# Output projection of a hybrid encoder block: six of its eight chunks as seven block products

## The reference, cut to what matters

```python
D_MODEL, SEQ = 1024, 512
def layer(x):                                   # x: (512, 1024) float32
    h = rmsnorm(x, g_pre_mix)
    (..., gate_a, gate_b) = split_columns(h @ w_in)
    o_a, o_b = sparse_attention(...), stick_breaking_attention(...)
    m = (sigmoid(gate_a) * (o_a @ w_branch_sparse)
         + sigmoid(gate_b) * (o_b @ w_branch_sb))
    x = x + rmsnorm(m @ w_out, g_post_mix)      # <- the output projection
    h = rmsnorm(x, g_pre_ffn)
    g, u = split(h @ w_gate_up)
    return x + rmsnorm((silu(g) * u) @ w_down, g_post_ffn)
```

## Time and profile before

| | |
|---|---|
| median of three runs | 751.95 us |
| the profiled execution's own time | 751.47 us |
| its span, from first to last instruction | 749.7 us |
| PE busy | 741.4 us (99%) |
| DVE, ACT, POOL busy | 555.5, 427.9, 298.1 us |
| granted clock of TensorE, mean | 0.999 |

### The profile page before, as it was taken

How to read it: one execution, slowest core, us unless ns; L and a number is a source line. 1 busy time by engine, 2 the same in 40 slices (tenths; PEclk the granted TensorE clock), 3 DMA queues, 4 the chain that set the end, 5 groups by cost and what they waited for, 6 DMA issues and landing times.

```text
span 749.7 us, 11720 instructions
## 1 busy us (share of the span) xinstructions
PE 741.4 (99%) x4250; PEld 652.6 (87%) x4250; DVE 555.5 (74%) x781; ACT 427.9 (57%) x688; POOL 298.1 (40%) x213
## 2 busy tenths in 40 slices
PE   9999999999999999999999999999999999999996
PEld 7788888888888888888888989999999999788885
DVE  4979989977567565369607767778877777985778
ACT  5763177777677585643146454545554554655564
POOL 6937265966777878425382430000000000133102
PEclk9999999999999999999999999999999999999999
DMA  9652433213212232124553025323333314899902
GB/s 336 187 167 78 156 108 95 58 56 97 72 52 83 72 99 76 57 80 145 214 178 92 22 60 166 106 85 94 108 112 112 112 56 155 337 193 205 212 8 112
DMA packets 108977, 90.25 MB, mean 120 GB/s; under 512 B 3584, under 2 KB 91656, under 8 KB 108936
## 3 DMA queue, kind: packets, MB, share of 16 engines
q1 hardware_dynamic: 103752, 78.18, 33.3%
q0 software_dynamic: 4992, 11.54, 8.3%
q10 hardware_dynamic: 192, 0.01, 0.0%
HBM read 82.61 MB, written 3.68 MB: 115 GB/s over the span
## 4 chain that ended last, share of the span: by engine, by line
PE 95%; ACT 1%; DVE 1%; POOL 1%; issue 1%; DMA 0%; POOLq 0%; SPq 0%; ACTq 0%
PE ps L615 12%; PE ps L617 12%; PE ps L616 12%; PE ps L636 12%; PE ps L984 11%; PE ps L930 8%; PE ps L931 8%; PE ps L932 8%; PE ps L693 3%; PE ps L851 3%; PE ps L840 2%; PE ps L823 1%; PE ps L825 1%; ACT wr_hi L1436 1%; POOL x L1697 1%
## 5 line engine op out<-in xcount | busy, mean ns | idle before, releaser
L615 PE MATMUL ps<-h_hi,w_hi 128*128 128x512 f32 (+1 forms) x320 | 123.6, 386 | 0.0
L617 PE MATMUL ps<-h_hi,w_lo 128*128 128x512 f32 (+1 forms) x320 | 121.8, 381 | 0.0
L616 PE MATMUL ps<-h_lo,w_hi 128*128 128x512 f32 (+1 forms) x320 | 121.6, 380 | 0.0
L1688 POOL DMA_DIRECT2D w_a<-in_w_down x12 | 15.4, 1529 | 227.9 <-DVE xd_lo L2170 221.7
L1621 POOL TENSOR_TENSOR w_lo<-raw,w_hi 128x1024 fp32r<-128x1024 f32 x30 | 78.3, 2611 | 30.5 <-ACT w_hi L1180 30.1
L1505 POOL TENSOR_TENSOR w_lo<-raw,w_hi 128x1024 fp32r<-128x1024 f32 x20 | 48.7, 2441 | 58.1 <-ACT w_hi L1032 53.1
L617 PEld LDWEIGHTS ps<-h_hi,w_lo 128*128 128x128 f32 x320 | 60.2, 188 | 11.5
L616 PEld LDWEIGHTS ps<-h_lo,w_hi 128*128 128x128 f32 x320 | 60.4, 189 | 9.8
L615 PEld LDWEIGHTS ps<-h_hi,w_hi 128*128 128x128 f32 x320 | 60.3, 188 | 9.8
L2165 DVE TENSOR_TENSOR wr_lo<-w_a,wr_hi 128x1536 fp32r<-128x1536 f32 (+1 forms) x28 | 45.5, 1624 | 21.8 <-ACT wr_hi L1436 21.8
L930 PE MATMUL ps<-t_hi,sum_hi 128*128 128x256 f32 x216 | 61.1, 283 | 0.0
(11 more groups left out here) (284 smaller groups left out, 2163.2 us busy)
## 6 DMA issues: line engine op xcount, KB each, us to landing
raw<-in_w_in SPq DMA_DIRECT2D x40, 512.0 KB, 4.6
raw<-in_w_gate_up SPq DMA_DIRECT2D x26, 512.0 KB, 3.9
raw<-in_w_gate_up SPq DMA_DIRECT2D x36, 256.0 KB, 4.3
w_a<-in_w_down SPq DMA_DIRECT2D x9, 768.0 KB, 7.0
w_a<-in_w_down POOLq DMA_DIRECT2D x9, 768.0 KB, 10.1
raw<-in_w_out SPq DMA_DIRECT2D x8, 512.0 KB, 4.3
w_a<-w_a POOLq DMA_DIRECT2D x3, 768.0 KB, 13.2
x_t<-in_first SPq DMA_DIRECT2D x8, 256.0 KB, 6.6
```

The lines of the kernel that those rows point to most:

```text
L615: mm(acc, whi_c, a_hi_, start=first, stop=False)
L616: mm(acc, whi_c, a_lo_, start=False, stop=False)
L617: return mm(acc, wlo_c, a_hi_, start=False, stop=last)
```

## The change

The first six chunks of `m` and of `w_out` are treated as block matrices. `m` is cut in two halves of three chunks and, for tokens, in two halves of 256; `w_out` in two halves of three chunks and two halves of 512 columns. Each product of such blocks is then one of seven instead of eight, with sums of blocks as operands (`T1` to `T4` of `m`, `S1` to `S4` of the weights). The last two chunks are multiplied as before, by `last_chunks`. So PE runs 7 products of 18 matmuls and 48 matmuls for the last two chunks, 174 in all, where there were 192, all of 512 columns.

The sums of weights are made by DMAs issued from GpSimd that add to what lies in their destination. The sums of `m` are made by DVE in place. ACT rounds all blocks (`out_hi_of`) and keeps or copies partial sums in PSUM; DVE makes all low halves of the output stage (`out_rest_of`, `last_rest`) and the low halves of the first four up weights (`split_rest`). GpSimd makes the low halves of the branch weights only, issues four adding DMAs, and negates half of a gain row. The up weights' first load and the loads of `x` move to earlier places in SP's list. In `last_chunks` of block 3 the transpose of block 1 stands between its two chunks.

The numbers of semaphores that later stages wait for shift by constants (`OUT_PARTS`, `OUT_PRODUCTS`, `OUT_KEPT`, `OUT_SUMMED`, `OUT_T`, `OUT_IN`); those lines are left out of the diff.

```diff
+    A11, A12, T2, S2, T3, S3, A22, WL0, WL1, T4, T1, S1, S4 = range(1, 14)
+    plain = {A11: s_11, A12: s_12, S2: s_two, S3: s_11, A22: s_22, S1: s_one, S4: s_12,
+             T1: m_block(0, 0), T2: m_block(1, 1), T3: m_block(0, 1), T4: m_block(1, 0)}
+    out_halves = {A11: slot_v, A12: slot_j, S2: slot_o, S3: slot_v, A22: slot_j, S1: slot_o, S4: slot_j,
+              T1: (t1_hi, t1_lo), T2: (t2_hi, t2_lo), T3: (t3_hi, t3_lo), T4: (t4_hi, t4_lo)}
...
 # SP
-        for j in range(KC // 2):
+        for j in range(2):
             pair(T_BR // 2 + j, j, branch, branch_sb)
...
+        sp.wait_ge(tile_done, T_BR)
+        sp.dma_start(s_one[:, :, :], out_block(1, 0)).then_inc(block_in[0], 16)
+        sp.dma_start(s_11[:, :, :], out_block(0, 0)).then_inc(block_in[1], 16)
+        pair(T_BR // 2 + 2, 2, branch, branch_sb)
+        sp.dma_start(s_two[:, :, :], out_block(0, 0)).then_inc(block_in[2], 16)
+        sp.dma_start(s_12[:, :, :], out_block(0, 1)).then_inc(block_in[3], 16)
+        sp.dma_start(s_22[:, :, :], out_block(1, 1)).then_inc(up_in, 16)
+        pair(T_BR // 2 + 3, 3, branch, branch_sb)
+        sp.wait_ge(m_lo_done, 1)
+        for t in range(TB):
+            sp.dma_start(x1[:, t, :], x_rows[:, t, :]).then_inc(x_rows_in[t], 16)
...
 # PE
+        pe.wait_ge(acc_free, READ + FILL)
+        pe.wait_ge(mixed, KC - 1)
+        pe.wait_ge(m_lo_done, OC)
+        out_product((1, 3), m_parts(0, 0), A11, True)
+        pe.wait_ge(m_lo_done, 2 * OC)
+        out_product((0, 2), m_parts(1, 0), A12, False, lambda b: pe.wait_ge(product_kept, b + 1))
+        out_product((1, 3), out_halves[T2], S2, False)
+        out_product((1, 3), out_halves[T3], S3, False, lambda b: pe.wait_ge(product_kept, b + 3))
+        pe.wait_ge(parts_lo_done, T4)
+        out_product((1, 3), out_halves[T4], A22, False, lambda b: pe.wait_ge(product_kept, b + 5))
+        pe.wait_ge(m_lo_done, KC)
+        last_chunks(0)
+        pe.wait_ge(parts_lo_done, S1)
+        pe.wait_ge(mixed, KC)
+        for b in range(2):
+            out_part(4 + 2 * b, out_halves[T1], S1, b, True).then_inc(product_done, 1)
+            if b == 0:
+                last_chunks(1)
+        pe.wait_ge(parts_lo_done, S4)
+        for b in range(2):
+            pe.wait_ge(summed_up, 2 * b + 2)
+            out_part(4 + 2 * b, m_parts(1, 1), S4, b, False)
+            last_chunks(2 + b, (lambda: turn(1, y_buf)) if b else None)
+            if b == 0:
+                turn(0, y_buf)
...
 # GpSimd
-        with gp.Fori(T_BR // 2 + 1, T_OUT // 2 + 2) as d:
-            for u in range(2):
-                split(d, u)
...
+        split(T_BR // 2 + 1, 0)
+        split(T_BR // 2 + 1, 1)
+        gp.wait_ge(block_in[0], 16)
+        gp.dma_start(s_one[:, :, :], out_block(1, 1), accum_op=ALU.add).then_inc(block_added[0], 16)
+        gp.wait_ge(parts_lo_done, A11)
+        gp.dma_start(s_11[:, :, :], out_block(1, 0), accum_op=ALU.add).then_inc(block_added[2], 16)
+        split(T_BR // 2 + 2, 0)
+        gp.wait_ge(block_added[0], 16)
+        gp.wait_ge(block_in[2], 16)
+        gp.dma_start(s_two[:, :, :], s_one[:, :, :], accum_op=ALU.add).then_inc(block_added[1], 16)
+        split(T_BR // 2 + 2, 1)
...
```

More of the change, by code:

```diff
@@ L82 @@
 GROUP = 3
+OC = 3
 ENDS = (0, 3, 6, 9, PAIRED)
@@ new lines, in out_product, with last_chunks @@
+        def out_product(banks, x_, w, first, ready=None):
+            pe.wait_ge(parts_lo_done, w)
+            for b in range(2):
+                if ready:
+                    ready(b)
+                out_part(banks[b], x_, w, b, first).then_inc(product_done, 1)
+        def last_chunks(t, before=None):
+            for i in range(2):
+                if i and before:
+                    before()
+                c = 2 * OC + i
+                x_h, x_l = (m[:, c, t * P:(t + 1) * P] for m in (m_hi, m_lo))
+                for n in (1, 0):
+                    half = slice(n * 512, (n + 1) * 512)
+                    for k, (x__, w_) in enumerate(((x_h, wl_hi[i]), (x_h, wl_lo[i]), (x_l, wl_hi[i]))):
+                        ins = mm(bank(2 * t + n), x__, w_[:, half], start=False, stop=i == 1 and k == 2,
+                                 skip_group_check=True)
+            ins.then_inc(block_done, 1)
@@ L1280, in _ @@
             split((T_BR + c + 2) // 2, c % 2)
-        split(T_OUT // 2, 0)
-        split(T_OUT // 2, 1)
-        split(T_OUT // 2 + 1, 0)
-        split(T_OUT // 2 + 1, 1)
-        for c in range(KC // 2, KC):
-            sc.wait_ge(raw_in, (T_OUT + c) // 2 * 32 + 32)
-            sc.wait_ge(m_lo_done, KC)
-            run(wo_hi[:, c - KC // 2, :], raw[:, (T_OUT + c) % 4, :], ACT.Copy).then_inc(w_hi_done, 1)
+            if c == 1:
+                sc.wait_ge(m_lo_done, 1)
+                sc.wait_ge(block_in[1], 16)
+                out_hi_of(A11)
@@ L1291, in two_banks @@
+        third_kept(0)
+        sc.wait_ge(product_done, 6)
+        out_hi_of(S1)
+        third_kept(1)
+        sc.wait_ge(raw_in, T_UP // 2 * 32 + 64)
+        sc.wait_ge(product_done, 8)
+        for u in range(2):
+            run(wu_hi[:, u, :], raw[:, (T_UP + 2 + u) % 4, :], ACT.Copy).then_inc(w_hi_done, 1)
+        sc.wait_ge(product_done, 10)
+        out_hi_of(S4)
         def two_banks(t):
@@ L1321, in _ @@
         first_norm(1)
-        sc.wait_ge(raw_in, T_UP // 2 * 32 + 64)
-        for u in range(2):
-            run(wu_hi[:, u, :], raw[:, (T_UP + 2 + u) % 4, :], ACT.Copy).then_inc(w_hi_done, 1)
         second_norm(1)
@@ L2003, in second_norm @@
             norm_x1(t)
-        for t in range(2):
-            out_sum(t)
-            sum_x1(t)
-            second_norm(t)
+        out_sum(0)
+        sum_x1(0)
+        fifth_added(0)
+        second_norm(0)
+        out_sum(1)
+        sum_x1(1)
+        fifth_added(1)
+        second_norm(1)
         out_sum(2)
```

326 lines of the change are left out of this document (215 added, 111 removed).

## The result

| | before | after |
|---|---|---|
| median | 752.02 us (4 runs) | 757.31 us (4 runs, 757.2 to 758.03) |
| profiled execution, span | 751.47, 749.7 us | 757.2, 755.3 us |
| granted clock of TensorE, mean | 0.999 | 0.996 |
| ratio of the times | | 1.0073, 95% interval 1.0061 to 1.0085 |

The change made the kernel 5.3 us slower. The forecast was 754.5 us, slower by 2.6 from the median it started from, with a range up to 758.0. The sign is right, the time lies in the range, and half of the size is missing.

What follows compares the result with a forecast made beforehand. PE, busy 99% of the span, was taken to bound the kernel. Terms -4.08 + 3.5 + 2.1 + 1.1 = +2.6 us took the median of 751.95 to 754.5 us; own range 753.1 to 757.6, 8 in 10 within 752.0 to 758.0.

Steps and rivals of the forecast that it cites:

- Matmuls removed: Output stage: 18 fewer matmuls, 174 instead of 192, at 0.2268 us each, worth -4.08 us.
- The wait at chunk 4: Branch stage: PE waits for GpSimd's split, held by A11's low half and the s_11 DMA; +3.5 us, bounds 3.4 to 5.0.
- Chunk 5's split and the landing of s_one: Branch stage: s_one's adding DMA likely lands at 345.1, the split ends at 348.6, PE needs it at 350.5; cost 0.
- The rival of a late landing: Branch chunk 5: s_one's adding DMA lands at 349.9, weights come 2.9 us late, time 757.4 us; chance 0.12.
- Chunks 6 and 7 go as before, 3.5 us later: Branch stage: no further wait at its last two chunks, stage ending at 366.8; cost 0.
- the loads go out while GpSimd and PE do other work, and each has over 5 us before its first reader: Moved and new loads: claimed to cost nothing.
- The clock: Rival: PE's idle 3.5 us at chunk 4 lowers the clock for some 3.5 us of matmuls; +1.75, 756.3 us, chance 0.06.
- DVE against PE in the output stage: PE waits at S2 (0.3), S3 (0.3) and A22 (1.5); together +2.1 us, bounds 1.0 to 3.3.
- h_lo: Ahead of the up projection: PE waits for transposed block 1's h_lo with only one chunk between; +1.1 us, 0.8 to 1.4.
- The signs: Expected in the profile: PE waits at chunk 4, A22 and the up projection, DVE's chunk 2 sum 0.7, output stage 44.5 us.

Runs made afterwards that it cites:

- Run 1: Changed kernel with GpSimd's split of chunk 4's low half moved ahead of the wait for A11 and the adding DMA into s_11: 760.32 us, ratio 1.0105.
- 8: Changed kernel with the adding DMAs issued only after the last branch weights landed, the third between the splits of chunks 6 and 7: 755.41 us, ratio 1.0048.
- 9: Run 8's kernel with the transpose of block 1 ahead of both chunks of block 3: 753.87 us, ratio 1.0028.
- 10: Run 8's kernel with both low-half splits of chunks 6 and 7 ahead of the DMA into s_two: 754.07 us, ratio 1.0023.
- 11: Run 10's kernel with the transpose of block 1 ahead of both chunks of block 3: 752.72 us, ratio 1.0006.
- 12: Run 11's kernel with loads of s_12 and s_22 behind the third pair of branch weights, adding DMAs started one at a time among the splits: 751.66 us.
- run 4: Changed kernel with sixteen extra matmuls, result unused, on PE ahead of its wait for chunk 4's weights: 757.4 us, ratio 1.0065.
- 2: Changed kernel with SP's four loads of x, and the load behind them, issued only when all branch weights have landed: 757.89 us, ratio 1.0072.
- 5: Changed kernel with SyncE issuing the second half of chunk 6's and 7's branch weights without waiting for the first half: 758.49 us, ratio 1.0079.
- 6: Run 5's kernel plus sixteen unused matmuls on PE ahead of chunk 4: 756.35 us, ratio 1.0058.
- 7: Changed kernel with GpSimd's four adding DMAs replaced by plain overwriting ones, so weight sums are left out: 757.65 us, one run only.

## Why the prediction was right, and where it was short

*Matmuls removed.* Right, to the matmul.

*The wait at chunk 4.* Right in mechanism, place and size (3.5 forecast, 3.84 measured): DVE's sum ran unheld, 0.69 us as forecast, and A11's low half ended at 341.63 against 341.35. Behind it GpSimd issued from 341.95, and the split began at 342.79 and took 2.82 where 2.40 was assumed. Run 1 confirms the cause, since with the split first the wait is gone.

*Chunk 5's split and the landing of s_one.* Right: forecast at 345.1, and GpSimd's next DMA, which waits for it, goes out at 345.55; chunk 5 had no wait. The rival of a late landing did not come up at 10.5 us. In runs 8 to 12, where the DMA stood beside other transfers, it landed in 12.2 to 14.1 us, and in all five PE waited for what came behind it.

*"Chunks 6 and 7 go as before, 3.5 us later", and "the loads go out while GpSimd and PE do other work, and each has over 5 us before its first reader".* This is the step that failed. It looked at the new loads' own readers, and not at what they do to loads that are already there. The traffic had been seen: the rival of a late landing counts 2 MB of x and 1 MB of branch weights, but only as a burden on the adding DMA, and not the other way round. The branch weights 6 and 7 have no slack of their own to spare: SyncE issues them in two pairs with a wait between, so a load slowed from 3 to 10 us counts twice. They arrived at 355.87; before, at 338.5 + 3.0 = 341.5, some 14 us earlier. In the changed kernel the wait at chunk 4 hides all but 1.15 us of that, but it is the stronger bound: run 1 took away the wait and run 4 the lost clock, and neither got anything.

*The clock.* It was a rival at 0.06, put that low because at the end of the run the clock held for 2.8 us without a matmul. The wait here was 3.68 us, the clock fell, and the rival's price, +1.75, was the measured 1.9. The end of the run was a bound from below and the forecast used it as if it covered 3.5 us as well. The Trainium skill, TensorE: Matmul & The Clock Gate, section on what is actually happening, has the lower level as the default that activity releases; here the trace agrees, with 0.62 and 0.58 in the two windows behind the wait, and 1.00 in run 4, where matmuls filled it. But the term was priced on top of the rest, and run 4 shows that as long as chunk 6's weights bound, giving the clock back gained nothing.

*DVE against PE in the output stage.* +2.1 forecast, 0.67 measured, with the same places: S2's wait did not appear, S3's was 0.3, A22's 0.36 instead of 1.5. The estimate was right for a kernel without the wait at chunk 6: in runs 2, 5, 6 and 7, where chunk 6 had none, A22 waited 1.48 to 1.52. The loads' delay lent DVE that time, so the two errors offset each other by 1.1 us. That part of the agreement is luck.

*h_lo.* Right: +1.1 forecast, 1.24 measured; the pairs of runs that moved the transpose differ by 1.5 (8 and 9) and 1.35 us (10 and 11).

*The signs.* The idle stretch at chunk 4, the DMA into s_11 behind A11's low half, the sum of 0.69 us and the wait for h_lo came as named. The wait of 1 to 2 us ahead of A22 did not, and the output stage took 43.45 us instead of 44.5.

So a sum of +2.6 became +4.9: two missing terms, 1.15 and 1.9, less 1.4 in the output stage, of which the first of them covered 1.1, plus 0.3, 0.1 and 0.2 of small ones. The measured time lies inside the stated range, but partly by luck: the upper end had been built from a longer wait at chunk 4 and longer ones in the output stage, and neither came. The order of the transfers and of the transpose was worth 757.31 - 751.66 = 5.6 us. But even in the best order found here, where two adding DMAs in a row took 14.1 and 9.0 us, more than half of what 18 matmuls gave (2.3 of 4.08) was paid back. Not tried were an ACT list with the copies of A11's banks ahead of S2's high half, loads of x behind the DMA into s_one, and sums of weights made by an engine.

## What to carry to other kernels

Where PE is busy all the time, a change that adds transfers has to be priced on the loads that are already in flight: for each existing load in that window, ask how late it may land before its reader stands, and count twice one that the queue's own wait chains to another. Removing one wait of several in a row shows only the next bound; before forecasting the gain from it, look up when the next supplier would be ready if PE came early. And a new idle stretch of 3 to 4 us on PE should be priced with a fall of the clock: here each one from 3.15 us up had it.
